# Differential-attention score products of both maps issued together, with a FoX weight split and the RWKV state transpose moved

## The reference

```python
# FoX, 8 heads of 64: softmax(q k / 8 + d_q - d_k, causal) v
# differential attention, 4 heads, two maps c of head size 64 each, values of 128
s = jnp.einsum('bqhcd,bkhcd->bhcqk', qb, k_all) * scale
p = softmax(where(kpos // 64 <= qpos // 64, s, -inf))
o = einsum('bhqk,bkhv->bqhv', p[:, :, 0] - lam * p[:, :, 1], v_all)
# RWKV-7, 8 heads, state S of 64 x 64
S = S * w + sa * (kk * a) + v * k ;  y = S r
```

## Time and profile before

| what | us |
|---|---|
| median of 3 runs | 3007.36 |
| lowest of them | 3005.76 |
| the profiled execution | 3008.48 |
| its span in the profile | 3006.7 |
| TensorE busy in the span | 2861.5 (95%) |
| VectorE, ScalarE busy | 1637.3 (54%), 746.2 (25%) |

### The profile page before, as it was taken

How to read it: one execution, slowest core, us unless ns; L and a number is a source line. 1 busy time by engine, 2 the same in 40 slices (tenths; PEclk the granted TensorE clock), 3 DMA queues, 4 the chain that set the end, 5 groups by cost and what they waited for, 6 DMA issues and landing times.

```text
span 3006.7 us, 63127 instructions
## 1 busy us (share of the span) xinstructions
PE 2861.5 (95%) x26468; PEld 2644.9 (88%) x26468; DVE 1637.3 (54%) x3027; ACT 746.2 (25%) x1789; POOL 243.6 (8%) x423
## 2 busy tenths in 40 slices
PE   7999999999999989999989999999999999899998
PEld 6877788999999789999988777799999997899998
DVE  4444554666674356664364445546666633566633
ACT  1133333323233330000112333342222323200001
POOL 1111111000000100000001211120000000000000
PEclk9999999999999999999989998899999999999999
DMA  4443345222163223332224434362222531233331
GB/s 123 125 131 99 98 130 138 83 79 73 39 185 98 60 80 89 87 88 86 78 78 134 114 96 121 98 161 72 78 62 65 175 98 43 85 88 88 87 86 62
DMA packets 420762, 290.26 MB, mean 97 GB/s; under 512 B 38544, under 2 KB 386352, under 8 KB 420352
## 3 DMA queue, kind: packets, MB, share of 16 engines
q1 hardware_dynamic: 398496, 228.64, 27.3%
q0 software_dynamic: 21984, 57.59, 6.0%
HBM read 232.12 MB, written 54.07 MB: 95 GB/s over the span
## 4 chain that ended last, share of the span: by engine, by line
PE 81%; DVE 9%; ACT 3%; DVEq 3%; issue 2%; DMA 2%; ACTq 0%; SPq 0%
PE PS L714 33%; PE PS L781 10%; PE PS L1077 7%; PE PS L1019 7%; PE PS L692 4%; PE PS L946 2%; PE PS L1226 2%; DMA U<-gate_scratch 2%; ACT U L1333 1%; PE PS L657 1%; PE PS L1056 1%; PE PS L863 1%; PE PS L828 1%; ACT U L1336 1%; PE PS L730 1%
## 5 line engine op out<-in xcount | busy, mean ns | idle before, releaser
L714 PE MATMUL PS<-U_r,WHI 128*128 128x272 f32 x2656 | 475.4, 290 | 18.0 <-DVEq L1833 9.2
L1336 ACT COPY U<-PS 128x272 f32<-128x272 f32 (+9 forms) x756 | 263.3, 372 | 752.4 <-PE PS L1077 140.0
L1822 DVE CAST WHI<-ring 128x1024 fp32r<-128x1024 f32 (+1 forms) x240 | 164.2, 684 | 512.4 <-PE PS L714 379.2
L714 PEld LDWEIGHTS PS<-U_r,WHI 128*128 128x128 f32 x2656 | 387.2, 189 | 23.3 <-DVEq L2250 10.8
L714 PE MATMUL PS<-brT_r,WHI 128*128 128x272 f32 x1728 | 357.5, 288 | 0.0
L714 PE MATMUL PS<-U_r,WLO 128*128 128x272 f32 x1696 | 351.2, 289 | 0.0
L714 PE MATMUL PS<-hT_r,WHI 128*128 128x272 f32 x1696 | 351.1, 289 | 0.0
L1832 DVE TENSOR_TENSOR WLO<-ring,WHI 128x1024 fp32r<-128x1024 f32 (+1 forms) x240 | 289.8, 1208 | 19.0 <-issue 0.9
L781 PE MATMUL PS<-U_r,WHI 128*128 128x272 f32 x832 | 268.2, 322 | 15.8 <-ACT U L1336 15.7
L714 PE MATMUL PS<-brT_r,WLO 128*128 128x272 f32 x1344 | 278.2, 288 | 0.0
L714 PEld LDWEIGHTS PS<-brT_r,WHI 128*128 128x128 f32 x1728 | 271.7, 188 | 0.2
(11 more groups left out here) (328 smaller groups left out, 4470.6 us busy)
## 6 DMA issues: line engine op xcount, KB each, us to landing
ring<-in_w_in_dram SPq DMA_DIRECT2D x126, 512.0 KB, 4.2
ring<-in_w_ffn_in_dram SPq DMA_DIRECT2D x88, 512.0 KB, 3.8
ring<-in_w_ffn_out_dram SPq DMA_DIRECT2D x32, 448.0 KB, 3.7
proj_scratch<-U POOLq DMA_DIRECT2D x104, 136.0 KB, 2.0
U<-proj_scratch SPq DMA_DIRECT2D x48, 272.0 KB, 4.4
ring<-in_w_branch_dram SPq DMA_DIRECT2D x48, 256.0 KB, 3.3
gate_scratch<-U POOLq DMA_DIRECT2D x88, 136.0 KB, 3.1
U<-gate_scratch SPq DMA_DIRECT2D x44, 272.0 KB, 2.9
```

Of the source, the lines that this page charges most:

```text
L714: ins = mm(PS[:, 2 * q + h, 0:HT], w, half(x, h), start=(first and k == 0 and n == 0), stop=(last and k == kn - 1 and n == len(terms) - 1))
L1336: return act.copy(out, in_)
L1822: copy(hi, src)
```

## The change

It issues the two maps' score products of a tile one behind the other and then the two masks; it moves the second FoX weight split from step 8 to step 9; and it transposes the RWKV sample state before stage 1, copies it there, and puts the evacuations of stage 10 of groups 1 and 2 between the first steps of the chain.

```diff
@@ scores(p), TensorE @@
-                            for c in range(2):
-                                r = slice(64 * c, 64 * c + 64)
-                                b = 2 * c if i == 4 else 2 * ((p + 1) % 2) + c
-                                if i < 4:
-                                    n = (i + 1) * P
-                                    mm(PS[:, b, 0:n], DQ[h][r, i * P:(i + 1) * P], DK[h][r, 0:n], start=True,
-                                       stop=False)
-                                    ins = mm(PS[:, b, n - P:n], identb[:, :], mdiffb[:, :], start=False, stop=True)
-                                else:
...
-                                ins.then_inc(df_scores, 1)
+                            maps = [(c, slice(64 * c, 64 * c + 64), 2 * c if i == 4 else 2 * ((p + 1) % 2) + c) for c in range(2)]
+                            if i < 4:
+                                n = (i + 1) * P
+                                for c, r, b in maps:
+                                    mm(PS[:, b, 0:n], DQ[h][r, i * P:(i + 1) * P], DK[h][r, 0:n], start=True, stop=False)
+                                for c, r, b in maps:
+                                    mm(PS[:, b, n - P:n], identb[:, :], mdiffb[:, :], start=False, stop=True) \
+                                        .then_inc(df_scores, 1)
+                            else:
+                                for c, r, b in maps:
+                                    mm(PS[0:32, b, :], DQ[h][r, SEQ:T], DK[h][r, T:T + PAST], start=True, stop=True)
+                                for c, r, b in maps:
+                                    mm(PS[0:32, b + 1, 0:32], DQ[h][r, SEQ:T], DK[h][r, SEQ:T], start=True, stop=True) \
+                                        .then_inc(df_scores, 1)
@@ TensorE, RWKV pass @@
                         sums(W_RAW[:, 2, :]).then_inc(rw_sum, 1)
+                        halves = (slice(0, 64), slice(64, 128))
+                        eye = const("stack")[:, 0:64]
+                        for r in halves:
+                            ins = mm(PS[r, 5, 256:320], ST[r, 11, :], eye[r], start=True, stop=True)
+                        ins.then_inc(rw_state, 1)
                         both(q0 + 2, it)
...
-                        halves = (slice(0, 64), slice(64, 128))
-                        eye = const("stack")[:, 0:64]
-                        for r in halves:
-                            ins = mm(PS[r, 5, 256:320], ST[r, 11, :], eye[r], start=True, stop=True)
-                        ins.then_inc(rw_state, 1)
@@ VectorE, FoX @@
-                        if k in (3, 8):
-                            late_split(3 * it + k // 8)
+                        if k in (3, 9):
+                            late_split(3 * it + k // 9)
@@ VectorE, RWKV pass @@
                             tt(BON[:, c], PS[:, 2 + 2 * s, 0:TP // 2], Vx[:, c], ALU.mult)
+                        dve.wait_ge(rw_state, g * 10 + 1)
+                        copy(ST[:, 8, :], PS[:, 5, 256:320]).then_inc(rw_chain, 1)
                         dve.drain()
...
-                        for s in range(1, 11):
+                        for s in range(1, 10):
                             for gr in range(3):
                                 evac(s, gr)
-
-                        dve.wait_ge(rw_state, g * 10 + 1)
-                        copy(ST[:, 8, :], PS[:, 5, 256:320]).then_inc(rw_chain, 1)
-                        dve.drain().then_inc(rw_free, 1)
+                        evac(10, 0)
                         for c in range(9):
                             dve.wait_ge(rw_state, g * 10 + c + 2)
...
+                            if c < 2:
+                                evac(10, c + 1)
+                            if c == 1:
+                                dve.drain().then_inc(rw_free, 1)
```

More of the change, by code:

```diff
@@ L940, in scores @@
                                 pe.wait_ge(df_exp, g * 20 + 10 * h + (1 if p == 1 else 2 * p - 2))
-                            for c in range(2):
-                                r = slice(64 * c, 64 * c + 64)
-                                b = 2 * c if i == 4 else 2 * ((p + 1) % 2) + c
-                                if i < 4:
-                                    n = (i + 1) * P
-                                    mm(PS[:, b, 0:n], DQ[h][r, i * P:(i + 1) * P], DK[h][r, 0:n], start=True,
-                                       stop=False)
-                                    ins = mm(PS[:, b, n - P:n], identb[:, :], mdiffb[:, :], start=False, stop=True)
-                                else:
+                            maps = [(c, slice(64 * c, 64 * c + 64), 2 * c if i == 4 else 2 * ((p + 1) % 2) + c) for c in range(2)]
[8 more added lines that the diff above has]
+                                for c, r, b in maps:
                                     mm(PS[0:32, b, :], DQ[h][r, SEQ:T], DK[h][r, T:T + PAST], start=True, stop=True)
-                                    ins = mm(PS[0:32, b + 1, 0:32], DQ[h][r, SEQ:T], DK[h][r, SEQ:T], start=True,
-                                             stop=True)
-                                ins.then_inc(df_scores, 1)
+                                for c, r, b in maps:
+                                    mm(PS[0:32, b + 1, 0:32], DQ[h][r, SEQ:T], DK[h][r, SEQ:T], start=True, stop=True) \
+                                        .then_inc(df_scores, 1)
                         def turn(p):
```

## The result

The changed kernel took 2957.95 us (median of four runs: 2953.61, 2957.47, 2958.43, and one outlier of 5503 us) beside 3009.19 us for the kernel before (four runs, one of them the outlier of 15319 us): a ratio of 0.9826, 95% interval 0.9808 to 0.9843. A second series of four runs had a median of 2954.90, ratio 0.9817 (0.9799 to 0.9834). The forecast was 2947.0, with 2936 to 2974 as its range. So the kernel is 1.7 to 1.8% faster, 51 us by the two medians of the 61 that were forecast. The profiled execution took 2953.61 us, 4 us under the median, with a span of 2951.8; against the 3008.48 of the one before it saves 54.9 us.

What follows compares the result with a forecast made beforehand. TensorE, carrying 81% of the chain that ended last, was taken as the bound. Savings of 27.1+28.6-1.5+7.0+0 = 61.2 us off 3008.48 gave 2947; the 8-in-10 range was 2936 to 2974.

Steps and rivals of the forecast that it cites:

- Part 1: Differential-attention scores: both maps' half-height products run side by side, saving 3.39 us per head, 27.1 us in all.
- rival C: Score products don't run side by side; only 64 changes of height go, 6.4 us, giving about 2994; chance 0.04.
- New waits: Differential steps of 128 and 256 columns: less score work covers ScalarE's copy of the late product, costing 1.5 us.
- Part 2: Both differential-attention stages: the clock rises from 0.91 and 0.90, winning 28.6 of 32.6 us.
- Rival D: Shorter scores open gaps at late copies, TensorE falls to 1.2 GHz for whole heads, 3043 us; chance 0.03.
- half-clock time T costs T/2: Price of the low clock: time T at 1.2 GHz costs half of T; T was put at 65 us.
- 4 kept back: 4 us of the 32.6 us clock gain left out for the unchanged stretch ahead of the 384-column tile.
- rival B: Differential stages' clock keeps falling: 2975 us, or 2959 if half the lost clock comes back; chance 0.25.
- Not for want of work: Differential stages: the clock falls though TensorE is busy all the while, 4.00 us of 4.00 in the fourth head.
- Part 3: FoX: the weight split a step later removes TensorE's waits for a late bank copy, 7.4 us; 7 taken.
- Part 4: RWKV, 8 passes: earlier chain start gains 3.6 us, moved products cost 3.2; taken as 0, bounds -3 and +4.
- 0.45 are left at step 2: RWKV chain: of 1.1 us gained at step 0, 0.45 remain at step 2, 3.6 us over 8 passes.

Runs made afterwards that it cites:

- same-half: Changed kernel with the second map's score product also contracting rows 0 to 63, so the two products can't overlap: 2980.83 us, ratio 0.9905.
- full-rows: Kernel before, each score product of tiles 0 to 3 contracting all 128 rows in place of its own 64: 2977.42 us, ratio 0.989.
- The last three kernels: Changed kernel with late quarter before step 3's wait; that plus ScalarE's evacuation before the exponentials; or only turn(0) before step 2's late quarter: 2953.72, 2961.90, 2944.95 us.
- Evacuation first: Changed kernel with step 3's late quarter ahead of the wait and ScalarE's late_put ahead of that step's exponentials: 2961.90 us, ratio 0.9836.
- Late quarter first: Changed kernel with step 3's late quarter issued ahead of the wait for tile 0's turned probabilities: 2953.72 us, ratio 0.9817.
- The last kernel: Changed kernel with turn(0) ahead of step 2's late quarter and ScalarE's copy of it ahead of tile 2's exponentials: 2944.95 us, ratio 0.9783.

## Why the prediction was right, and where it was off

**Part 1 (27.1 us): right in sum, wrong in its price for the order.** The tiles give 26.5 us (3.31 per head). "Do they run beside each other?" was answered yes, from the earlier trace rows, and the 512-column tile took 1.17 us for the forecast 1.2. But rival C priced the changes of height at 0.1 for each of 64, 6.4 us, and without any overlap they were worth 9.6: 32 excursions at 0.30.

**New waits (1.5 us): right in size, partly in the wrong place.** I put them on ScalarE's copies; the DMA wait at L908 alone grew by 1.6 us in two layers, and L981's by 0.1 to 0.3 a layer. The transfer was in the trace of before, 0.6 us late, and I had not asked what shorter heads would make of it. The slack of the last tile came out as forecast (its combination ends at 330.05 us, its transposes start at 330.90), but it was not the tightest: the 384-column tile was, with 0.05 us. Rival D's "gaps are under 0.6 us" overlooked waits of TensorE of up to 1.0 us at L781 in the same stage; they brought no fall. At one clock the scores alone give 29.0, 4 more than 26.5-1.6; that is more than its error of 2.1, and I leave it open (the one slope for all kernels may be a part of it).

**Part 2 (28.6 us of clock): the step that failed, in size.** Its direction held: 0.98 in both stages, which the text had set at 0.97 or more. Over the runs, though, the mean clock rose from 0.9786 to 0.9854, worth 6.8 x 2.39 = 16.2 us. Three things make the 12 us. First, "half-clock time T costs T/2": 0.001 of mean clock is 6 us at the low clock (0.002 of 3000) and cost 2.39, so a microsecond at the low clock costs 0.40, not 0.50 (0.44 by the two traces of one stage); that waits and latencies do not stretch with the clock would explain it, but no run isolates this. That turns 32.6 into 26. Second, the falls at the 384-column tile stayed in half of the heads; 0.02 of 311 us at 0.8 of its price is 5 us, near the 4 kept back. Third, the clock fell a little more elsewhere: the traces have it low for 62 us outside these stages before and 64 to 67 after. The rest of the gap is within what the runs scatter. The time that came out is nearer to rival B's "half of the lost clock comes back", 2959, than to the forecast. B was right in part: its "low stretch ahead of the 384-column tile stays" is what half of the heads showed, though the falls at 512 columns went. That the total came as near as it did is partly luck, since 4.0 us too little for the chain made up for a third of what was too much for the clock.

The reason given, half the rows idle for microseconds, was shown in part, and one reading under it was wrong. "Not for want of work: TensorE is busy all the while" rests on the earlier trace rows, which lies inside a fall; what tells why a clock fell stands ahead of it, and there, in 452 to 456 us, is the wait of 0.54 us. The text knew that stretch and kept 4 us back for it, but every fall of the stage began behind it. By the Trainium skill, page "TensorE: Matmul & The Clock Gate", section "Why this matters for your kernels", a fall is put down to gaps. This case's traces agree that a gap stands ahead of each fall. The same-half and full-rows kernels speak against gaps as the whole: with the waits in place the mean clock is 0.9823 and 0.9856, for 0.9854 in the changed kernel and 0.9786 before. The last three kernels speak for a share of them: the two without a wait ahead of the 384-column tile and with no wait over 1.5 us elsewhere had no fall in these stages, and the one with waits of 1.9 us had its falls right behind them. A wait and half-height work behind it pull together; which share each has is open, since no run has the old order without the wait.

**Part 3 (7.4 us, took 7): right.** 6.9 us in the stages, 7.0 +- 1.2 in the kernel by itself, and the row of waits went from six to two.

**Part 4 (0 us, bounds -3 and +4): 4 us too low, at its own upper bound.** The steps of the chain came where they were put (1.49, 2.5 and 3.6 us after the first evacuation in the forecast; 1.44, 2.37 and 3.40), and the transposes beside the gate cost 0.43 us per pass for the 0.4 forecast. The step that failed is "0.45 are left at step 2": the comparison ended there. Stage 11 of the first group waits for the second step only, not for the third, so TensorE runs it while VectorE still evacuates, and 0.94 us are left at it and at what follows it. 0.94-0.43 = 0.5 per pass, 4 us.

**The sum.** 26.5-1.6 for the scores, 7.0, 4.0 and 16.2 make 52; the medians differ by 51 to 56. The forecast's 61.2 had 12.4 too much for the clock and 4.0 too little for the chain.

## What to carry to other kernels

When a chain of short steps is reordered, follow it to the first instruction that needs only a part of it: that one, not the last step compared, tells what is left. Before moving an instruction to cover a wait, see what is queued behind the place it goes to; two of three attempts here moved the wait to the next reader, and the one that worked put nothing ahead of the head of the softmax chain. And where a clock steps between two levels, read every run's mean clock beside its time: a line through 118 runs told parts of 4 and 7 us from nothing and gave them an error of 1.2, where the runs of one kernel spread over 20 us and more. To find why a clock fell, read what the engine did ahead of the fall, not within it.

## What the runs showed of the hardware that was not expected

- Products on rows 0 to 63 and on rows 64 to 127 start 6 to 7 ns apart and overlap in full: both maps take the time of one, 1.13 us for 1.12.
- A group of half-height products between full-height ones costs about 0.3 us in all: 0.63 us from product to mask at 256 columns against 0.43 on full rows, and 0.16 against 0.06 from mask to product.
- The low clock costs 0.40 us per microsecond in this kernel, by the line through all runs, or 0.44, by two traces of one stage, not 0.50.
- Every fall in the differential stages begins 1.3 to 3.7 us after a wait of 0.5 to 0.8 us (46 falls behind 72 waits), or within 1.2 us of one of 1.9 us (four, in "Evacuation first"); waits of 1.2 to 1.5 us at another place ("Late quarter first") brought none.
- The same code in the same stage was granted 0.91 in one execution and 0.97 in another, and runs of one kernel spread over 27 us with it. The five runs of the last kernel, which has no fall left in its differential stages, lie within 1.8 us: 2943.82 to 2945.60.
